# A weight sum one split later, and sums of activations one step sooner, in a two-layer decoder trunk on one core

## The reference

```python
def swiglu(h, w_gate, w_up, w_down):
    return (jax.nn.silu(h @ w_gate) * (h @ w_up)) @ w_down
...
    for layer in range(DEPTH):
        h = rms_norm(x, mix_norm[layer])
        ...
            mix = hybrid_ab_mixer(h, ab_w_in[i], lower_bounds[i], hg_out_norm[i], ab_w_out[i])
        ...
            mix = multiscale_pool_mixer(h, pool_w[i], pool_scale[i])
        x = x + mix.astype(x.dtype)
        h = rms_norm(x, ffn_norm[layer])
        x = x + swiglu(h, ffn_w_gate[layer], ffn_w_up[layer], ffn_w_down[layer]).astype(x.dtype)
    return rms_norm(x, final_norm)
```

## Time and profile before

| | us |
|---|---|
| median of 3 runs | 1931.27 |
| lowest, highest | 1929.78, 1931.37 |
| profiled execution | 1929.66 |
| its span, first to last instruction | 1927.9 |
| PE busy in the span | 1911.1 |
| DVE busy | 1478.9 |
| ACT busy | 955.6 |

### The profile page before, as it was taken

The page is one execution under the profiler, slowest core; times in us unless marked ns, Lnnn a source line. Parts: engine busy times, 40 slices in busy tenths (PEclk is TensorE's granted clock), DMA queues, the critical chain, the costliest instruction groups (busy, mean ns, idle before and its releaser), DMA issues.

```text
span 1927.9 us, 21995 instructions
## 1 busy us (share of the span) xinstructions
PE 1911.1 (99%) x9224; PEld 1601.9 (83%) x9224; DVE 1478.9 (77%) x1099; ACT 955.6 (50%) x746; POOL 23.6 (1%) x85
## 2 busy tenths in 40 slices
PE   9999999999999999999999999999999999999998
PEld 7889999988788888888888888878888888888886
DVE  6656788865987687786887877788589687786895
ACT  6444334435554454453554556655346354454463
POOL 1000000000000000000000030000000000000000
PEclk9999999999999999999999999999999999999999
DMA  9555444454476467565474675457557467575582
GB/s 312 179 175 165 153 153 152 143 185 155 138 253 240 137 238 258 193 244 196 174 273 143 243 266 169 150 176 263 195 196 248 145 221 261 183 255 198 192 284 88
DMA packets 216987, 385.12 MB, mean 200 GB/s; under 512 B 6001, under 2 KB 55234, under 8 KB 216642
## 3 DMA queue, kind: packets, MB, share of 16 engines
q1 hardware_dynamic: 216672, 383.29, 58.2%
q10 hardware_dynamic: 226, 0.55, 0.1%
HBM read 381.72 MB, written 2.10 MB: 199 GB/s over the span
## 4 chain that ended last, share of the span: by engine, by line
PE 83%; DVE 12%; ACT 2%; issue 1%; DMA 1%; SPq 0%; DVEq 0%; ACTq 0%
PE main L1628 33%; PE main L1634 17%; PE main L1570 8%; PE aux L1650 7%; DVE lo L1005 6%; DVE raw L1011 5%; PE main L1572 4%; PE aux L1654 3%; PE main L1650 3%; PE main L1654 2%; ACT hi L640 2%; PE aux L1577 1%; PE aux L1739 1%; PE main L1681 1%; PE main L1682 1%
## 5 line engine op out<-in xcount | busy, mean ns | idle before, releaser
L640 ACT CAST hi<-raw 128x2048 fp32r<-128x2048 f32 (+1 forms) x401 | 764.3, 1907 | 741.2 <-PE main L1634 401.4
L1005 DVE TENSOR_TENSOR lo<-raw,hi 128x2048 fp32r<-128x2048 f32 x328 | 745.9, 2289 | 249.4 <-ACT hi L640 249.2
L1628 PE MATMUL main<-hi,act 128*128 128x512 f32 x1712 | 407.6, 391 | 0.0
L1628 PE MATMUL main<-hi,mid 128*128 128x512 f32 x1632 | 389.7, 391 | 0.3 <-DVE mid L1273 0.2
L1628 PEld LDWEIGHTS main<-hi,act 128*128 128x128 f32 x1712 | 320.2, 188 | 66.0 <-DVE act L1305 0.2
L1628 PEld LDWEIGHTS main<-hi,mid 128*128 128x128 f32 x1632 | 304.7, 188 | 64.6 <-DVE mid L1273 1.7
L1570 PE MATMUL main<-act,hi 128*128 128x512 f32 x640 | 229.1, 402 | 0.0
L996 DVE TENSOR_TENSOR lo<-raw,hi 128x2048 fp32r<-128x2048 f32 x71 | 162.6, 2290 | 79.4 <-ACT hi L640 79.4
L1634 PE MATMUL main<-lo,act 128*128 128x512 f32 x856 | 211.5, 389 | 0.0
L1634 PE MATMUL main<-lo,mid 128*128 128x512 f32 x816 | 201.6, 389 | 0.0
L1634 PEld LDWEIGHTS main<-lo,act 128*128 128x128 f32 x856 | 160.7, 188 | 33.3
(11 more groups left out here) (190 smaller groups left out, 1415.0 us busy)
## 6 DMA issues: line engine op xcount, KB each, us to landing
raw<-in_ffn_w_gate SPq DMA_DIRECT2D x108, 1024.0 KB, 5.3
raw<-in_ffn_w_up SPq DMA_DIRECT2D x88, 1024.0 KB, 6.5
raw<-in_ffn_w_down SPq DMA_DIRECT2D x88, 1024.0 KB, 5.1
raw<-in_ab_w_in SPq DMA_DIRECT2D x55, 1024.0 KB, 5.1
raw<-in_ab_w_out SPq DMA_DIRECT2D x16, 1024.0 KB, 5.1
raw<-in_pool_w SPq DMA_DIRECT2D x4, 1024.0 KB, 5.5
xn<-in_x SPq DMA_DIRECT2D x4, 512.0 KB, 8.2
raw<-in_ab_w_in SPq DMA_DIRECT2D x2, 512.0 KB, 6.3
```

What stands on the lines that cost most here:

```text
L640: return nc.scalar.copy(out_, in_)
L1005: V.tensor_tensor(lo[:, split_at(t), :], src, hi[:, split_at(t), :].bitcast(F32), ALU.subtract).then_inc(lo_ready, 1)
L1628: mm(o2[:, h, :], lhs[:, k0 + n, c, h * P:(h + 1) * P], w_hi, start=(first and c == 0 and n == 0), stop=False)
```

## The change

The fourth weight sum moves behind the remainder of slot 4, and the release number of b11's place, which that sum reads, from s + 4 to s + 5. In layer 0 the first set of activation sums is begun in the last slots of the output projection (the j loops over `S_OUTA`) and finished there; the second set is made in the slots b = 1 and 2 instead of b = 3 and 4. In layer 1 the first set is made at b = 0 and 1 (before: 1 and 2), the second at b = 2 and 3 (before: 3 and 4). No instruction's size or number changes.

```diff
@@ places()
-            free += [(b22.at, s + 3), (b11.at, s + 4), (b12.at, s + 5), (b21.at, s + 6)]
+            free += [(b22.at, s + 3), (b11.at, s + 5), (b12.at, s + 5), (b21.at, s + 6)]
@@ ACT, output projection
                 elif j > 0:
                     keep_x(T_OUT + j // 2 - 1, j // 2 - 1, V_FFN, 0)
+                if j == 7:
+                    sums_hi(0, 0)
@@ ACT, start_of_layer
-                if b == 2:
-                    sums_hi(layer, 0)
-                if b == 4:
+                if b == 1 and layer == 1:
+                    sums_hi(1, 0)
+                if b == 2 + layer:
                     sums_hi(layer, 1)
@@ DVE, prepare
-                if i == 2:
+                if i == 3:
                     loaded(3)
                     ve.wait_ge(sum_made, BLOCK_SUMS * block_index(s0) + 3)
                     add(3, 0)
@@ DVE, output projection
+                if j == 6:
+                    sums_of(0, 0)
+                if j == 7:
+                    sums_lo(0, 0)
@@ DVE, start_of_layer (the first four new lines stand in the branch of layer 1)
-                if b == 1:
-                    sums_of(layer, 0)
-                if b == 2:
-                    sums_lo(layer, 0)
-                if b == 3:
+                    if b == 0:
+                        sums_of(1, 0)
+                    if b == 1:
+                        sums_lo(1, 0)
+                if b == 1 + layer:
                     sums_of(layer, 1)
-                if b == 4:
+                if b == 2 + layer:
                     sums_lo(layer, 1)
```

## The result

The changed kernel takes **1935.33 us** (median of 9 runs, 1934.51 to 1936.29); beside it, on the same chip, the kernel before took 1929.82 (9 runs, 1928.32 to 1931.37). The ratio is 1.0029, 95% interval 1.0020 to 1.0037: 5.5 us slower. The forecast was 1938.1, between 1930 and 1946. The span of the profiled execution went from 1927.9 to 1933.7.

A forecast was written before the change was run, and what follows sets the result against it. The prediction took TensorE (PE), busy 1911.1 of 1927.9 us, as the bound, so only its waits count. Its terms, -9.6 + 11.6 + 4.8 = +6.8 us on the median of 1931.27, gave 1938.1 us, range 1930 to 1946.

The forecast's parts named there:

- The gain, 9.6 us: PE's waits for remainders vanish: 4.9 us at fourth products in 18 blocks, 4.7 at the layers' starts.
- Rival (c): At the layers' starts the backlog only moves on, 4.7 us not gained: +11.5 us, 1942.8; chance 10%.
- the fifth and sixth splits: Behind the moved fourth sum on DVE: both still in time for PE, nothing lost.
- x1's landing, 5.4 us after its issue: Second extra product's load in second blocks: issued 2.20 us later, lands after 5.4 us, bounds 5.1 and 6.5.
- Rival (d): Two loads issued together share the engines, x1 (second extra product) lands after 6.0 us or more: +12.8, 1944; chance 10%.
- rival (b): Loads after a second block come about as early as before, so all 9.6 us stay: 1921.7; chance 8%.
- The estimate of 4.4 us: Skill's landing for a 1 MB load; x1 (second extra product) would cost 0.16 us, the sum be about -3.
- x1's cost, 11.6 us: The second extra product, waiting for its late load's splits, costs PE 1.16 us in each of ten second blocks.
- The single terms: At the second extra product PE waits 0.65 us for ACT's split and 0.51 for DVE's.
- The chain to the hidden tile, 4.8 us: Later loads delay the hidden tile's remainder before the down projection: four groups lose 1.0 us, four 0.2.
- the two signs by which the prediction called itself wrong: PE doesn't stop at the second extra product; or the hidden tile's remainder is in time despite loads 2 us later.
- The sum: Whole kernel: -9.6 + 11.6 + 4.8 = +6.8 us, median 1938.1 us; this forecast's chance 52%.

The follow-up runs named there:

- sums_only: Kernel before with only the activation sums made sooner, fourth weight sum and b11's release unmoved: 1924.99 us beside 1930.56, ratio 0.9971.
- fourth_by_sum: Kernel before with the fourth sum moved and b11's load waiting for that sum's own count, activation sums unmoved: 1925.72 us beside 1929.49, ratio 0.9979.
- by_sum: Changed kernel, but b11's load waits for the fourth sum's own count and split 4, not split 5: 1922.01 us beside 1930.56, ratio 0.9957.
- release_only: Kernel before with only b11's release moved from s + 4 to s + 5, the sum unmoved: 1942.04 us beside 1929.88, ratio 1.0063.
- late_rest: by_sum with b12's place released at s + 6 instead of s + 5: 1927.61 us beside 1929.49, ratio 0.9991.
- release_six: Changed kernel with the places of b11 and b12 released at s + 6: 1969.39 us beside 1929.88, ratio 1.0202.

## Why the prediction was right, point by point

**The gain, 9.6 us.** Shown. The stops that were to go add up to 9.4 us in the trace of before and are gone in after; the two halves measured 5.6 (sums_only) and about 4 (fourth_by_sum), and together 8.5 (by_sum). Rival (c), that the backlog only moves on at the layers' starts, is out: there is no stop left in the rows of both starts above. Nothing showed at the new places of the sums; the fifth and sixth splits were in time, as worked out.

**x1's landing, 5.4 us after its issue.** In after the ten landings took 5.13 to 5.46 us, 5.28 in the mean. Rival (d), landing after 6.0, is out, rival (b) too: the load behind it doesn't hurry it, but doesn't slow it much either. The estimate of 4.4 us from "DMA: Bandwidth & Descriptors" in the Trainium skill, by which the change would have come out without a loss, fits these ten landings no better than those in the trace of before.

**x1's cost, 11.6 us.** The trace has 6.6 + 4.8 = 11.4. The single terms were 0.65 and 0.51, and the block shown has 0.71 and 0.51. (The 854.28 of the second term should be 851.96 + 2.29 = 854.25; that is 0.3 us in ten blocks.) That the cause is the release, and neither the sum nor its place on DVE, is shown by release_only (the release without the sum: 12.2 us of loss, with ten waits at x1) and by by_sum (the sum without the release: none of it).

**The chain to the hidden tile, 4.8 us.** This term was mis-sized, and its reason only half right. At the down projection after has 0.7 us more than before, not 4.8. The step that failed is that in four of the eight groups PE waits for the hidden tile already and so loses all of 1.0: the four waits of before cost PE little in starts (0.3 and 0.4 in two groups, about 0.1 or nothing in the rest), and PEld's idle time is not PE's. In the group of the earlier trace rows PEld idles 0.23 us in after, and PE loses 0.1. Nor is it a matter of fixed groups: the one that lost 0.3 in before (1492.62) loses 0.1 in after. Of the two signs by which the prediction called itself wrong, the second has mostly come: the hidden tile's remainder is in time, or nearly, in six of the eight groups, in spite of loads 2 us later. The late loads were paid for elsewhere: 1.8 us more at `hi` parts with `act`, most of it in two groups whose first up load took about 9 us, and 0.9 at one turn. Together 3.3 against 4.8. In all three groups one load landed 3.9 to 4.3 us behind the load ahead of it, where 2.7 is usual. Before has such loads in the same three groups, 4.0 to 4.6 us behind, and loses nothing at these places: there x1 and the loads behind it landed some 2 us sooner, measured against PE's products. That the stops come from the lateness of the loads is made likely by this and by late_rest, which leaves x1's load in time, delays those behind it and has stops of the same kinds; why single loads are slow isn't known.

**The sum.** Forecast +6.8, measured +5.5 in the medians, +5.8 in the spans: -9.4 + 11.4 + 3.3 = +5.3 by the stops. The predicted median is 2.8 us too high, half for the chain's term, half because the kernel before measured 1929.82 this time and not 1931.27.

## What to carry to other kernels

When a step that frees a buffer is moved, look for the transfer that the buffer's release starts, and for the queue behind it, before counting what the step itself gains; here 9.4 us were won and 14.7 spent. Release a buffer by the count of its last reader, not by the next event that happens to stand behind it: that one wait turned 5.5 us of loss into 8.5 us of gain. The waits listed for the weight loads are not what the matmuls lose (x1's `hi` part in after: 8.1 us listed, 6.6 lost): measure the distance between the matmuls' starts.

## What the runs showed of the hardware

A stop of PE can cost more than its length. In release_six the granted clock falls to its lower level behind some of the long stops at x1. Two of the ten, the third and the fourth:

```profile
861.10 2.11 PE L1656 MATMUL aux<-hi,act 128*128 128x512 f32 x8 [2.61 <-ACT hi L640]
863.43 1.19 PE L1660 MATMUL aux<-lo,act 128*128 128x512 f32 x4 [0.22 <-DVE lo L1007]
```

```profile
992.26 2.76 PE L1656 MATMUL aux<-hi,act 128*128 128x512 f32 x8 [2.79 <-ACT hi L640]
994.83 1.91 PE L1660 MATMUL aux<-lo,act 128*128 128x512 f32 x4
996.53 3.81 PE L1634 MATMUL main<-hi,act 128*128 128x512 f32 x15
```

At 863.43 the four matmuls begin after DVE has finished and, from the second on, follow each other at the usual 0.227 us. At 994.83 four take 1.70 us until the next row begins, 0.43 us each, which is 0.20 more for each of eight or so matmuls, about 1.6 us for this stop. It happened behind six of the ten stops, those of 3.04, 2.95, 2.68, 3.84, 2.81 and 3.96 us in starts, and not behind those of 2.74, 2.77, 2.84 and 2.96: their length alone doesn't decide it in this range, and what does stayed open. No stop of before and after in the last stages, at most 1.8 us, had it, and the mean granted clock is 0.999 in both against 0.994 here:

```profile
core 0: 1965.6 us, clock 0.994
```

So the price of a late load is not a straight line: 2.2 us more on ten loads cost 23 us by the stops at x1 and another 9.5 by the clock.
